# The first token tile's way into the expert layer, moved into the recurrence

## The reference, cut to what matters

```
x = x + concatenate([o_a, o_b], axis=-1) @ w_out          # o_a: attention, o_b: recurrence, 512 columns each
x = x + peer_ffn(rmsnorm(x, norm_ffn), p_wq, p_keys, p_u, p_v)

# peer_ffn, a block of 128 tokens
q = (xb @ w_q).reshape(128, 8, 2, 64)                      # 8 heads, two half queries
sc = einsum('thpd,hpnd->thpn', q, keys)                    # against 128 keys for each half
s1, i1 = top_k(sc[:, :, 0], 16); s2, i2 = top_k(sc[:, :, 1], 16)
top_s, top_pos = top_k(s1[..., :, None] + s2[..., None, :], 16)
eidx = the expert's number, i1 * 128 + i2 at top_pos       # of 16384 experts
h = gelu(einsum('td,thkd->thk', xb, u_tab[eidx]))
out = einsum('thk,thkd->td', softmax(top_s) * h, v_tab[eidx])
```

```
sa = S @ a_t;  S = S * w_t + sa b_t^T + v_t k_t^T;  y_t = S @ r_t
out = (layernorm(y) + bonus) * g
```

## Time and profile before

| | us |
|---|---|
| median of three runs | 3643.26 (3641.67 to 3647.87) |
| the profiled execution | 3646.62 |
| its span, first to last instruction | 3644.7 |
| PE busy | 3008.7 (83%) |
| DVE busy | 2588.9 (71%) |
| ACT busy | 1343.4 (37%) |
| POOL busy | 1436.8 (39%) |
| DMA moved | 1293.40 MB, mean 355 GB/s |

### The profile page before, as it was taken

The page is one execution under the profiler, slowest core; times in us unless marked ns, Lnnn a source line. Parts: engine busy times, 40 slices in busy tenths (PEclk is TensorE's granted clock), DMA queues, the critical chain, the costliest instruction groups (busy, mean ns, idle before and its releaser), DMA issues. The chain is left out here.

```text
span 3644.7 us, 38367 instructions
## 1 busy us (share of the span) xinstructions
PE 3008.7 (83%) x11628; PEld 1432.9 (39%) x11628; DVE 2588.9 (71%) x6361; ACT 1343.4 (37%) x4033; POOL 1436.8 (39%) x1241
## 2 busy tenths in 40 slices
PE   8997878887777778999898888988988877777777
PEld 5765763333323223444344333333434322222222
DVE  2675647876666667798988577999777666666664
ACT  3354213333333333236653232345623333333332
POOL 1200004544444445454445354544444444444443
PEclk9997998999999999999999999999999999999999
DMA  4101039999999999999999999999999999999998
GB/s 133 39 15 47 3 99 419 417 414 421 406 421 422 402 422 396 419 416 380 339 413 404 390 414 419 421 416 342 417 421 421 412 417 416 422 421 405 422 421 352
DMA packets 216573, 1293.40 MB, mean 355 GB/s; under 512 B 23600, under 2 KB 41008, under 8 KB 68784
## 3 DMA queue, kind: packets, MB, share of 16 engines
q0 software_dynamic: 165888, 1208.03, 80.7%
q1 hardware_dynamic: 50480, 82.93, 6.5%
HBM read 1286.49 MB, written 3.87 MB: 354 GB/s over the span
## 5 line engine op out<-in xcount | busy, mean ns | idle before, releaser
L1592 PE MATMUL banks<-ring,route 128*128 128x512 f32 (+1 forms) x4184 | 2019.4, 619 | 529.1 <-ACT route L1577 507.3
L1500 POOL DMA_INDIRECT ring<-in_uv,route x1152 | 1329.1, 1154 | 1679.7 <-PE banks L1592 1537.6
L1511 DVE SCALAR_TENSOR_TENSOR ring<-ring,XN 128x1024 f32<-128x1024 f32 x1152 | 1425.8, 1238 | 742.9 <-DMA ring<-in_uv,route 726.5
L1592 PEld LDWEIGHTS banks<-ring,route 128*128 128x128 f32 (+1 forms) x4184 | 740.9, 188 | 1640.6 <-issue 852.7
L1562 ACT ACTIVATE route<-route 128x2 f32<-128x2 f32 x576 | 117.2, 204 | 1834.6 <-DVE ring L1511 1834.1
L1577 ACT ACTIVATE route<-IDN,route 128x128 f32<-128x128 f32 x918 | 317.0, 387 | 4.2 <-PE banks L1592 3.3
L1567 ACT ACTIVATE route<-route 128x1 f32<-128x1 f32 x1152 | 276.6, 287 | 23.2
L1920 PE MATMUL banks<-own,QP 128*128 128x512 f32 (+1 forms) x400 | 177.6, 569 | 2.9 <-ACT QP L2011 2.2
L1562 ACT ACT_TABLE_LOAD x106 | 136.0, 1283 | 1.9
L1521 DVE SCALAR_TENSOR_TENSOR X<-ring,route,X 128x1024 f32<-128x1024 f32 x106 | 135.8, 1281 | 0.0
L1920 PEld LDWEIGHTS banks<-own,QP 128*128 128x128 f32 x400 | 77.1, 193 | 92.3 <-issue 83.7
(11 more groups left out here) (450 smaller groups left out, 3114.2 us busy)
## 6 DMA issues: line engine op xcount, KB each, us to landing
ring<-in_uv,route POOLq DMA_INDIRECT x1152
own<-in_l_w_in SPq DMA_DIRECT2D x16, 1024.0 KB
own<-in_l_w_out SPq DMA_DIRECT2D x12, 1024.0 KB
own<-in_l_peer_wq SPq DMA_DIRECT2D x12, 1024.0 KB
X<-in_x_prompt SPq DMA_DIRECT2D x8, 512.0 KB, 6.1
ring<-in_l_w_in SPq DMA_DIRECT2D x4, 1024.0 KB, 9.8
ring<-in_l_peer_wq SPq DMA_DIRECT2D x2, 2048.0 KB, 12.4
own<-in_l_w_in SPq DMA_DIRECT2D x4, 656.0 KB
```

Source lines behind the costliest of these rows:

```text
L1500: pool.indirect_dma_start(self.ring[:, s % RING, :], None, self.io[f"uv{of_slot(s)[0]}"], bass.IndirectOffsetOnAxis(ap=self.EI[:, g % 2, k ...
L1511: dve.scalar_tensor_tensor(u, u, 1.0, self.XN[:, of_slot(s)[1], :], ALU.mult, ALU.mult, accum_out=self.HD[:, g % 2, k:k + 1]).then_inc(sel ...
L1592: m = pe.matmul(self.bank[1 + half][0:n, :], self.DG[:, (V_TENSOR[s] - 1) % 4, 0:n], self.ring[:, s % RING, D + 512 * half:D + 512 * half ...
```

## The change

Token tile 0's way to its first key scores moves into the recurrence. The four transposes of OC go to tau 44, the 16 products to taus 46 to 57 (one at a time in the first eight). The residual (DVE, taus 54 and 58), the squares (ACT, 58), the mean (DVE, 59), the root (GpSimd), the scaling to `XN0` (DVE, 60), the eight transposes (PE, 61), their copies (ACT, 62) and the queries of heads 0 and 1 (PE, taus 63 and 64; ACT 64 and 65) follow. On PE they stand ahead of the youngest chunk's stage of that tau, on ACT and DVE behind it. The gain, the weights of these two heads and their keys are loaded at the start of the recurrence. These values lie in free parts of `own` and of the ring (`FirstTile`). The tail begins with the key scores of groups 0 and 1; ACT copies X of tile 0 from the ring to its place, and only then SP issues the query weights of heads 2 and 3 and what follows; DVE copies XN behind the first search. PE makes the six other heads' queries behind the keys' arrival. The output weights wait for these queries.

```diff
+class FirstTile:
+    def __init__(self, side):
+        room = Room(side[:, 2624:])
+        self.XT, self.QP = room.take(KD, P), room.take(2, P)
+        room = Room(side[:, 4096:])
+        self.GM, self.ss = room.take(D), room.take(NT)[:, 4:5]
+        self.XN, self.KB = room.take(D), room.take(2, 2 * NK)
...
-        FIRST = {56: [(0, 0), (0, 1)], 57: [(0, 2), (0, 3)], 58: [(1, 0), (1, 1)], 59: [(1, 2), (1, 3)],
-                 60: [(0, 4), (0, 5)], 61: [(0, 6), (1, 4)], 62: [(1, 5), (1, 6)], 63: [(0, 7)], 64: [(1, 7)]}
+        order = [(b, k) for b in range(2) for k in range(8)]
+        FIRST = {46 + i: order[i:i + 1] for i in range(8)} | {54 + i: order[8 + 2 * i:10 + 2 * i] for i in range(4)}
+        youngest = {tau: c for tau, c, k in turns}
         def first_tile(pe, tau):
-            if tau == 54:
+            if tau == 44:
...
+            if tau == 61:
+                pe.wait_ge(xn.h, xn.at(1))
+                for b in range(2):
+                    for k in range(4):
+                        m = pe.transpose(bank[6 + b][:, k * P:(k + 1) * P], XN0[:, (4 * b + k) * P:(4 * b + k + 1) * P], ident)
+                    m.then_inc(tr.h, 1)
+            if tau in (63, 64):
+                h = tau - 63
+                if h == 0:
+                    pe.wait_ge(xt.h, xt.at(2))
+                    pe.wait_ge(gl.h, gl.at(64))
+                for k in range(KD):
+                    m = pe.matmul(bank[6 + h][:, 0:P], WQ2[:, k, h * P:h * P + P], XT0[:, k, :],
+                                  start=(k == 0), stop=(k == KD - 1))
+                m.then_inc(qm.h, 1)
+        def first_tile_act(act, tau):
+            if tau == 45:
+                act.wait_ge(ot.h, ot.at(1))
+                act.activation(OCT, bank[6], ACT.Copy).then_inc(oc.h, 1)
+            elif tau == 58:
+                act.wait_ge(ad.h, ad.at(2))
+                act.activation(XN0, X0, ACT.Square, accum_out=ss0).then_inc(sq.h, 1)
+            elif tau == 62:
+                for b in range(2):
+                    act.wait_ge(tr.h, tr.at(1 + b))
+                    act.activation(XT0[:, 4 * b:4 * b + 4, :], bank[6 + b].rearrange("p (k n) -> p k n", k=4),
+                                   ACT.Copy).then_inc(xt.h, 1)
+            elif tau in (64, 65):
+                h = tau - 64
+                act.wait_ge(qm.h, qm.at(h + 1))
+                act.activation(QP2[:, h, :], bank[6 + h][:, 0:P], ACT.Copy).then_inc(ev.h, 1)
+        def first_tile_dve(dve, tau):
+            if tau in (54, 58):
+                b = (tau - 54) // 4
+                q = slice(b * 512, (b + 1) * 512)
+                dve.wait_ge(xf.h, xf.at(16))
+                dve.wait_ge(fo.h, fo.at(b + 1))
+                dve.tensor_tensor(X0[:, q], bank[7 - b], X0[:, q], ALU.add).then_inc(ad.h, 1)
+            elif tau == 59:
+                dve.wait_ge(sq.h, sq.at(1))
+                dve.tensor_scalar(ss0, ss0, 1.0 / D, EPS, ALU.mult, ALU.add).then_inc(mn.h, 1)
+            elif tau == 60:
+                dve.wait_ge(gl.h, gl.at(64))
+                dve.wait_ge(rt.h, rt.at(1))
+                dve.scalar_tensor_tensor(XN0, X0, ss0, GM, ALU.mult, ALU.mult).then_inc(xn.h, 1)
...
-                through(6)
-                sp.dma_start(XF[:, 2560:3584], io["x_prompt"][0, 0:P, :]).then_inc(xf.h, 16)
+                sp.dma_start(X0, io["x_prompt"][0, 0:P, :]).then_inc(xf.h, 16)
+                sp.dma_start(GM, io["l0_norm_ffn"].partition_broadcast(P)).then_inc(gl.h, 16)
+                sp.dma_start(WQ2, wqv[:, :, 0:2 * P]).then_inc(gl.h, 16)
...
+                    if c == last:
+                        pool.wait_ge(mn.h, mn.at(1))
+                        pool.tensor_tensor(ss0, ss0, IDN[:, 128:129], ALU.pow).then_inc(rt.h, 1)
                     roots.give(pool, c, ys[:, 1, :])
...
+                    if (c, k) in ((0, 17), (1, 17)):
+                        dve.wait_ge(dve_chain.h, dve_chain.at(ch.n))
+                        dve.engine_nop().then_inc(ob.h, 1)
+                    if c == youngest[tau]:
+                        first_tile_dve(dve, tau)
...
         def _(sp):
-            sp.dma_start(rest.GM, io["l0_norm_ffn"].partition_broadcast(P)).then_inc(gl.h, 16)
             wqv = io["l0_peer_wq"].rearrange("(k p) n -> p k n", p=P)
-            sp.dma_start(WQ[:, :, 0:512], wqv[:, :, 0:512]).then_inc(wq[0].h, 16)
+            sp.wait_ge(xd.h, xd.at(1))
+            sp.dma_start(WQ[:, :, 2 * P:512], wqv[:, :, 2 * P:512]).then_inc(wq[0].h, 16)
             sp.wait_ge(kz.h, kz.at(1))
...
-            sp.wait_ge(ad.h, ad.at(2))
...
+            sp.wait_ge(qm.h, qm.at(PH - 2))
+            sp.wait_ge(ex.scored.h, 2)
             rest.sp(sp)
...
         def _(pe):
-            pe.wait_ge(xn.h, xn.at(1))
...
+            ex.pe_route(pe, 0)
+            ex.pe_route(pe, 1)
+            pe.wait_ge(kl.h, kl.at(64))
+            for i in range(PH - 2):
+                h = i + 2
+                if h in (2, 4):
                     pe.wait_ge(wq[h // 4].h, wq[h // 4].at(16))
...
         def _(act):
...
+            ex.act_copy(act, 0)
+            act.activation(X[:, 0, :], first.X, ACT.Copy).then_inc(xd.h, 1)
             ex.act_exp(act, 0)
             ex.act_copy(act, 1)
+            for i in range(PH - 2):
+                act.wait_ge(qm.h, qm.at(i + 1))
+                act.activation(QP[:, 0, i + 2, :], bank[3 + i % 4][:, 0:P], ACT.Copy).then_inc(ev.h, 1)
...
             for _ in ex.dve_route(dve, ch, 0):
                 pass
+            dve.tensor_copy(XN[:, 0, :], first.XN).then_inc(nd.h, 1)
+            dve.wait_ge(nd.h, nd.at(1))
+            dve.wait_ge(xd.h, xd.at(1))
```

More of the change, by code:

```diff
@@ L333, in encoder @@
                   prefetch, zero)
-        rwkv(nc, io, sb, sig, bank, CST, BV, MIX, PC, lw, W2A, G2, IDN, wide, side, PA, PB, OC, OBT, X)
+        first = FirstTile(side)
+        rwkv(nc, io, sb, sig, bank, CST, BV, MIX, PC, lw, W2A, G2, IDN, wide, side, PA, PB, OC, OBT, X, first)
         l0.close()
         lo.close()
-        tail(nc, io, sb, sig, bank, ident, IDN[:, 128:129], X, own, ring, OC, OBT)
+        tail(nc, io, sb, sig, bank, ident, IDN[:, 128:129], X, own, ring, OC, OBT, first)
 V_END = KT7 * AH * AV
@@ L756, with rwkv @@
 V_W0, V_A0, V_KK, V_KA, V_RK, V_LG, V_LB, V_MU = 0, 4, 8, 12, 16, 20, 24, 28
-def rwkv(nc, io, sb, sig, bank, CST, BV, MIX, PC, lw, W2A, G2, IDN, wide, side, PA, PB, OC, OBT, X):
+def rwkv(nc, io, sb, sig, bank, CST, BV, MIX, PC, lw, W2A, G2, IDN, wide, side, PA, PB, OC, OBT, X, first):
     ident, eps = IDN[:, 0:128], IDN[:, 129:130]
@@ L1244, in rwkv @@
         ot, oc, fo, xf = (sig(n) for n in ("heads_turned", "heads_copied", "first_out", "first_x_loaded"))
[L1245 to L1247 removed]
+        ad, sq, mn, rt, xn, tr, xt, qm, ev = (sig(n) for n in (
+            "added", "x_squares", "x_means", "x_roots", "x_normed", "x_turned", "x_copied", "lifted", "lifted_copied"))
+        early = Room(wide[:, first_end:])
+        OCT, X0, WQ2 = early.take(512), early.take(D), early.take(KD, 2 * P)
+        XT0, GM, ss0, XN0, QP2, KB2 = first.XT, first.GM, first.ss, first.XN, first.QP, first.KB
+        first.X = X0
+        order = [(b, k) for b in range(2) for k in range(8)]
+        FIRST = {46 + i: order[i:i + 1] for i in range(8)} | {54 + i: order[8 + 2 * i:10 + 2 * i] for i in range(4)}
+        youngest = {tau: c for tau, c, k in turns}
         def first_tile(pe, tau):
[L1251 removed]
+            if tau == 44:
                 for k in range(4):
@@ L1301, in _ @@
                     act_stage(act, c, k)
-                    if (tau, c) == (55, last):
-                        act.wait_ge(ot.h, ot.at(1))
-                        act.activation(OCT, bank[6], ACT.Copy).then_inc(oc.h, 1)
+                    if c == youngest[tau]:
+                        first_tile_act(act, tau)
             @block.gpsimd
@@ L1327, in rwkv @@
         y_sig.end(NCH)
-        loaded.end(16), stored.end(32), zs.end(2), st_sig.end(NCH)
+        loaded.end(16), stored.end(32), zs.end(3), st_sig.end(NCH)
 SETS = ((0, 1, 4), (2, 3))
@@ L1393, in pe_route @@
         else:
-            m = pe.matmul(out, self.QP[:, t, h, :], self.KB[:, h, :], start=True, stop=True)
+            q, k = (self.first.QP, self.first.KB) if g < 2 else (self.QP[:, t, :, :], self.KB)
+            m = pe.matmul(out, q[:, h, :], k[:, h, :], start=True, stop=True)
         m.then_inc(self.scored.h, 1)
@@ L2483, in until, with tail @@
             yield m, x[1:]
-def tail(nc, io, sb, sig, bank, ident, half, X, own, ring, OC, OBT):
+def tail(nc, io, sb, sig, bank, ident, half, X, own, ring, OC, OBT, first):
     st = ExitStack()
@@ L2496, in tail @@
     WQ = whole.take(KD, D)
-    wq, gl = [sig(f"weights_loaded{i}") for i in (2, 3)], sig("gains_loaded")
-    xl, tr, mm_, ad, sq, mn, rt, xn, xt, qm, ev = (sig(n) for n in (
-        "first_x_loaded", "transposed", "first_out", "added", "squares", "roots_asked", "roots_done", "normed",
-        "evacuated", "lifted", "lifted_copied"))
```

(3 more changed lines are left out.)

65 lines of the change are left out of this document (19 added, 46 removed).

## The result

The kernel after takes 3656.15 us (median of 7 runs, 3654.14 to 3659.89), the kernel before, on the same chip, 3643.49 us (7 runs). The ratio is 1.0031 [1.0022, 1.0041], which is 11.3 us (8 to 15). The forecast was 3647.7 us, and within 7.3 us of no change with a chance of 0.61; 11.3 us are beyond that, a case to which the prediction gave 0.27. The profiled execution of after has a span of 3657.9 us, 13.2 longer than before's 3644.7, at a mean granted clock of 0.961 (0.967). It is the slowest of the seven (3659.89 us), 3.7 above their median; before's lies 3.1 above its own.

A forecast was written before the change was run, and what follows sets the result against it. The tail was taken as bound by DMA work, saturated from about 521.4 us. Recurrence +7.9, start +2.3, bytes removed -4.6, overlap -1.2, holes 0 gave +4.4 us: profiled 3651.0, median 3647.7 us; range 3638 to 3656.

The forecast's parts named there:

- What bounds the kernel: Tail: the end moves by transfer start, work added or removed, and idle DMA time, not by the first gather.
- The recurrence up to chunk 7's update: On PE: transposes +0.6, three exposed products +2.9, six products +3.2; the update begins at 496.4, 6.7 us later.
- The chain from there to chunk 8's update: Recurrence: waits for XN, transposes, stages, copies and query of head 0 take 20.8 us against 19.57, +1.2.
- From chunk 8's update to the barrier: Recurrence's end: second head's query lies beside the last chunk's norm and costs 0.
- Start of transfers behind the barrier: Tail: the first load waits for ACT's scores copy and copy of X, 2.2 to 2.5 us; +2.3 taken.
- Work removed: Tail: 1.57 MB of gain and query weights now load in the recurrence; -4.6 us, between 3.7 and 5.5 saved.
- Overlap: Tail: four gathers run beside the late small loads, at up to 422 GB/s; 0 to 2.3 us won, -1.2 taken.
- Holes: Tail: early gathers and output weights bridge the wait for queries and loads, so no DMA idle time; 0.
- The front: Tail: first gather 11.3 us after the barrier, at 539.6, 7.3 us earlier than before; by itself buys nothing.
- the front edge: Rival, 0.14: gathers through the eight-slot ring are the bound, so the end moves with gather 0; 3635.9 us.
- The waits absorb more: Rival, 0.14: the recurrence's waits hide the first eight products, barrier only 4 late, +0.5; 3643.8 us.
- The DMA engines run dry: Rival, 0.22: hole before gather 4, as queries at clock 0.50 end 7 us later; +8.9, 3652.2 us.

The follow-up runs named there:

- e2: Kernel after, but GpSimd waits for the six remaining queries ahead of gather 0 instead of gather 4; 3656.70 us, ratio 1.0035.
- e1: Kernel after plus 20 idle products on PE in front of its waits from tau 58 to 65, and one wait at tau 54; 3650.55 us, ratio 1.0019.
- e3: Kernel after with the moved 1.57 MB (gain, query weights of heads 0 and 1) loaded in the tail again; 3663.01 us, ratio 1.0054.
- e4: Kernel after with the other tiles' X loaded at once behind the barrier, before SP's wait for ACT's copy; 3663.54 us, ratio 1.0053.
- e9: Kernel after with the edits of e4 and e2 together: X loaded first, gather 0 waiting for the six queries; 3667.32 us, ratio 1.0059.
- e10: e8 with the gain and query weights of heads 0 and 1 (1.57 MB) loaded again in the tail; 3643.58 us, ratio 0.9998.
- e8: e7 plus six idle products on PE in taus 58 to 63 and the wait at tau 54 of e1; 3639.28 us, ratio 0.9986.
- e6: Kernel after with the 16 products spread singly over taus 15 to 45, later steps at taus 46 to 64; 3642.81 us, ratio 0.9998.
- e7: e6 with ACT copying X ahead of the key scores' copy in the tail; 3640.86 us, ratio 0.9991.

## Why the prediction was off, point by point

- *What bounds the kernel* (the ledger of DMA work): right. A late start of transfers carries the result, and a first gather 2.2 us earlier bought nothing. e2 settles it from the other side.
- *The recurrence up to chunk 7's update*: forecast 496.4, measured 496.75. That it agrees to 0.4 us is luck, since the same recurrence has this place anywhere from 494.06 to 497.78. The products cost 0.96 us each on PE where it was full, and the waits that were to absorb the others are down to 0.48 and 0.50 us.
- *The chain from there to chunk 8's update*, "With 0.1 for each of three handovers: ... = 20.8. Against 19.57: +1.2": **the step that failed**. It measured 24.75, +5.2. The order of waits was right (XN, transposes, stages 13 and 14, copies, query, update), but each price was taken at granted clock 1.00. The change takes the products out of taus 58 to 64, PE then waits in the recurrence's own stages, and the clock falls before the transposes begin: 1.97 us for 1.2, 3.78 for 1.8, stage 13 and the rest of that stretch likewise. e1 gives 20.5 at full clock. (The sum's last term is 0.1 where three handovers of 0.1 are named; with 0.3 and unrounded terms it is 20.9.) The row was at hand: 515 to 520 stood at 0.76 and 526 to 534 at 0.50 after idle time, and I used it for the rival's queries only. The Trainium skill (TensorE: Matmul & The Clock Gate, Part 1: The HAM clock gate) puts the ramp at under 1% of a typical kernel's span. The 4.4 us of e1 are 0.12% of this one, which agrees, but they are four tenths of the change's effect.
- *From chunk 8's update to the barrier*: 0 forecast, 11.83 us against 11.11, +0.7. PE was at the low clock there too (1.12 us for the turn); in e1 it is 11.12. Together the barrier came 13.0 us later, in e2, e3, e4 and e9 10.3 to 11.6, where 7.9 was forecast with bounds of 5 and 11.
- *Start of transfers behind the barrier*: +2.3 forecast, 2.63 measured.
- *Work removed*: -4.6 forecast. e10 against e8 says -4.3, with a small hole of e10 in it.
- *Overlap*: -1.2 forecast. The four gathers went through at 408 GB/s (546 to 558), but what was left of the small loads then ran at 345 (558 to 570) at a share of 1.01, no better than before's 340 in its mixed stretch. The balance of bytes leaves nothing to credit.
- *Holes*: 0 forecast. The share of 0.97 and 0.96 in 570 to 578 is 0.3 us.
- *The front*: first gather 11.3 us behind the barrier, as forecast to the tenth. The loads ended 35.4 us behind it, not 31 to 33; gather 4 came 26 us behind gather 0.

The sum with measured terms: 7.1 + 5.2 + 0.7 for the barrier, 2.6 for the start, -4.3 for the bytes, +0.3 for the hole: 11.6, where the ratio says 11.3. The agreement is closer than the terms are known. Of the two profiled executions, from which all these places come, the spans differ by 13.2, and with the barrier of e4 (530.65) the sum would be 8.9; with 3 us for the bytes it would be 1.3 more. The forecast's +4.4 lacks 4.0 of the chain, 0.7 behind it, 0.4 and 0.3 of the two starts, 1.2 of the overlap, 0.3 each of bytes and hole.

Of the rivals, the front edge (0.14) is refuted by e2. "The waits absorb more" (0.14) was wrong in the other direction. "The DMA engines run dry" (0.22) named the low clock and the sign, but put them in the tail. Its +8.9 is the nearest of all the figures, by another mechanism than the one that acted. In the kernel after the queries ended 24.6 us behind the barrier and were bridged; e3 and e4 show holes of 4 and 11 us, made in the main by query weights that landed late, with the clock only adding to them.

The range of 3638 to 3656 held by little: the ratio on the prediction's own starting median of 3643.26 gives 3654.6, while the measured median itself, 3656.15, is just beyond it. Its upper end was set for the "dry" rival and for a barrier 11 us late with a third of the other added, not for the sum, so that the time lies there owes something to luck.

Where the expected gain of such a move lies is shown by e8: the same work, put where PE waits in any case, costs the recurrence nothing (barrier at 517.38, before 520.37, and in e6, e7 and e10 at 517.27, 519.66 and 516.09). Of the 5.1 us won, 4.4 go when the 1.57 MB are loaded in the tail again (e10).

## What to carry to other kernels

When work is moved in front of a saturated stage, count when its transfers can start and how many bytes they carry, not when its first result is ready. When work that kept PE busy is taken out of a chain of waits, price what is left of the chain at the low clock as well as at the high one. Look for the loads that later transfers wait for by way of other engines: when they land late, the DMA engines can stand empty later, even if the first transfers started sooner (e4). Holding the early gathers back brought those loads in sooner, but did not shorten the kernel (e2, e9).

## What the runs showed of the hardware

- Idle products on PE shortened the kernel: 20 products of 128 x 256 in e1 gave 4.4 us; 6 in e8 gave 1.6 us by the medians, where the runs overlap too much to show it by itself.
- The same 16 instructions took 3.78 or 2.05 us with the granted clock, and which of them fell under the low clock differs between executions: in e2, with the same recurrence as after, query 0 took 2.05 us and the two updates were 22.6 us apart instead of 24.75. That is one source of the barrier's spread; a larger part arises before chunk 7's update, and its cause is open.
- Transfers of two queues shared the DMA engines: the same 2 MB of query weights took 21.5 us from issue to landing beside four gathers and 11.8 us without them (e4, e9).
- A DMA share of 1.0 is no rate. The same kernel ran at 272 GB/s (share 1.14), 345 (1.01) and 408 (1.03) in three neighbouring stretches. That the row sizes make the difference is likely, but no run varies them alone.
